# One f32 stack of a gated-attention/SSM mixer and an RWKV-7/sparse-attention block on one core: a three-stage join in the first mixer and four-corner matmuls in the state recurrence

## The chip, the cores and the metric

One Trainium2 chip, one NeuronCore in use. The metric is the device time of one execution in microseconds (us). TensorE (PE in the profile, with its weight loads as PEld), VectorE (DVE), ScalarE (ACT), GpSimd (POOL) and the queue of SyncE (SP) run their own instruction streams and meet on semaphores.

## The reference, cut to what matters

The change touches two parts. The first is the first mixer (512 tokens, 1024 channels), after its stick-breaking attention:

```python
proj = h @ w_in[layer]
q, k, v, z_attn, xbc, dt_raw, z_ssm = jnp.split(proj, splits, axis=-1)
...
y_attn = rms_norm(o, sb_norm_gain[layer]) * jax.nn.silu(z_attn)
xbc = jax.nn.silu(causal_depthwise_conv(xbc, conv_w[layer], conv_b[layer]))
dt = jax.nn.softplus((dt_raw + dt_bias[layer]).astype(jnp.float32))
y = ssd_scan(xs, dt, a, b_ssm, c_ssm, d_skip[layer])     # 4 chunks of 128 tokens, 16 heads
y_ssm = rms_norm(y * jax.nn.silu(z_ssm), ssm_norm_gain[layer])
mixed = jnp.concatenate([y_attn, y_ssm], axis=-1) @ w_out[layer]
x = x + gate[:, None, :] * mixed
```

`dt_raw`, the step sizes, is `h` times a 1024x16 part of the weights. The second is the recurrence of the RWKV-7 block (16 heads of 64 channels):

```python
def _wkv7_step(state, inp):
    r_t, w_t, k_t, v_t, a_t, b_t = inp
    sa = jnp.einsum('bhvk,bhk->bhv', state, a_t)
    state = (state * w_t[:, :, None, :] + sa[..., None] * b_t[:, :, None, :]
             + v_t[..., None] * k_t[:, :, None, :])
    y = jnp.einsum('bhvk,bhk->bhv', state, r_t)
    return state, y
```

The kernel computes it in 8 chunks of 64 tokens. Within a chunk the dependence of each token on those before it is a triangular 64x64 system for each head, and the kernel builds the inverse of its matrix in five levels of doubling.

## The kernel before

Everything lies in SBUF with channels on the 128 partitions, as tiles `F[i]` of 8 x 512 columns. Weights stream through `ring`, six slots of 512 KB that SyncE fills in a fixed `plan`; PE's `weight_used` frees a slot. All orders are written out by hand; no scheduler or planner moves an instruction.

**Split products.** Large f32 products run as three fp32r passes (`passes`, 128x512): weights and input are each split into a high part (a cast on ScalarE) and a low part (a subtraction). For one weight tile `t` of the joined first-mixer stream the chain is `high_of_weights(t)` on ScalarE into `w_high[t % 2]`, which has to wait until tile t-2 is done, then `low_of_weights(t)` (GpSimd from t = 2 on, L1337; VectorE for 0 and 1, L1244), then 24 passes on PE.

**The first mixer's stream (L1064 to L1343).** `w_dt` first: 32 f32 matmuls that hold 128 tokens of `h` as weights and stream 16 columns of `w_dt` (L1070). Then 12 convolution tiles, the first two interleaved by k, and 16 gate tiles `z_tile(j)`. The scan of four chunks is laid between gate tiles by `AFTER = [(1,2,3), (4,5,6), (7,8,9), (10,11,12)]`: chunk c's inputs, tile AFTER[c][0], its last broadcasts, the tiles AFTER[c][1] and AFTER[c][2], its outputs. ScalarE runs `chunk(c)` (its exponentials) whole and then `take_z` of the three tiles; `take_z(j)` also makes the high half of weight tile j+2. After `z_tile(13)` comes the sum of squares for the second norm, then tiles 14 and 15. GpSimd's `gate` multiplies the attention half by its gate.

**The output projection.** A new block `w_out` (`split_chain`, 16 weight tiles, 8 banks filled together). A block ends with a barrier of all engines; here ScalarE makes weights' and inputs' high halves, and VectorE both low halves and the final update of `x`.

**The recurrence (L1593 to L1846).** A round i handles chunks 2i and 2i+1 (x = 0, 1). `all_grams(i)` makes the Gram matrices and turns three tensors. Then for each level l: `q_level` (Q = N times G, L1663) for x = 0 and x = 1, and `g_level` for both: `GT += Q G`-like products into bank 3+2x (L1676) and, below level 5, `G`'s into bank 2+2x (L1680). Each is 8 pairs of heads x 2 halves = 16 f32 matmuls of 64x64, and each f32 matmul shows as two records in the profile, so 32 records. The two heads of a pair use partitions 0 to 63 and 64 to 127 of the inputs and the same of the output: two opposite corners of the array. VectorE takes every result (L1768 for Q, L1775 for GT, L1779 for G). Between the parts of the levels of round i stand the steps w, u, y, s of the previous round's two chunks (`carry`): w, u, y, s in levels 1 and 2, again in 3 and 4, none in level 5. GpSimd makes the start values (L1819 to L1823).

## Time and profile before

| | us |
|---|---|
| runs of the kernel before (3) | 2404.68, 2415.3, 2419.05; median 2415.3 |
| the profiled execution | 2409.52 |
| its span in the trace | 2407.7 |
| mean granted TensorE clock | 0.943 |

The profile is of one execution. Its span runs from the first to the last instruction of the program; the execution's own time is 1.8 us longer. Times of rows count from the start of the span. "Granted clock" is the share of the 2.4 GHz clock of TensorE: 1.0 is 2.4 GHz, 0.5 is 1.2 GHz. A matmul's end is modelled, so the distance from start to start says more of the rate than its duration.

### The profile page before, as it was taken

What the parts mean: (1) busy time and instruction counts of PE and PEld (TensorE: products, weight loads), DVE (VectorE), ACT (ScalarE), POOL (GpSimd) and SP (SyncE); (2) the same over time, 40 slices, a digit from 0 to 9 for tenths busy, and PEclk for the clock granted to TensorE, in tenths of its full rate; (3) what the DMA queues carried; (4) which work ended last, traced back from release to release, by engine and by line L of the source; (5) the groups of instructions that cost most, each with busy time, mean ns of one, the idle gap of its engine ahead of it and who ended that gap; (6) DMA issues with size and microseconds to landing.
All of it is one profiled execution on the core that took longest, in us unless ns stands there. A gap on an engine that the chain in (4) does not pass through costs nothing. (4 is left out here: it accounts for less than half of the span.)

```text
span 2407.7 us, 36981 instructions
## 1 busy us (share of the span) xinstructions
PE 2196.7 (91%) x16090; PEld 1677.4 (70%) x16090; DVE 1275.2 (53%) x1851; ACT 768.4 (32%) x1111; POOL 240.7 (10%) x171
## 2 busy tenths in 40 slices
PE   7998999988979966999899999899976988999898
PEld 3885777776858825999546788788434666888785
DVE  2335745554345475555435676733386536767434
ACT  2434653333223350000124222222244624222223
POOL 0000003233000043111310000000004400000000
PEclk9998989999989977999979999999887999999999
DMA  6221002111212200000101232322320021333231
GB/s 267 99 96 71 1 10 79 67 48 53 95 58 99 82 30 2 4 4 4 32 18 53 97 97 97 94 88 82 107 68 1 1 68 52 97 98 98 79 97 44
DMA packets 46850, 158.81 MB, mean 66 GB/s; under 512 B 5232, under 2 KB 7280, under 8 KB 46688
## 3 DMA queue, kind: packets, MB, share of 16 engines
q1 hardware_dynamic: 44832, 150.84, 19.1%
q10 hardware_dynamic: 1856, 5.60, 0.7%
q8 instruction: 127, 2.08, 0.3%
q14 instruction: 35, 0.29, 0.0%
HBM read 154.28 MB, written 2.14 MB: 65 GB/s over the span
## 5 line engine op out<-in xcount | busy, mean ns | idle before, releaser
L949 PE MATMUL banks<-up_x_high,up_w_high 128*128 128x512 f32 x672 | 262.1, 390 | 3.9 <-DVE up_w_low L920 3.9
L950 PE MATMUL banks<-up_x_low,up_w_high 128*128 128x512 f32 x672 | 262.1, 390 | 0.0
L951 PE MATMUL banks<-up_x_high,up_w_low 128*128 128x512 f32 x672 | 262.1, 390 | 0.0
L920 DVE TENSOR_TENSOR up_w_low<-weight_ring,up_w_high 128x1024 fp32r<-128x1024 f32 x88 | 107.8, 1226 | 129.8 <-ACT up_w_high L915 129.8
L915 ACT CAST up_w_high<-weight_ring 128x1024 fp32r<-128x1024 f32 x88 | 92.1, 1049 | 200.0 <-PE banks L951 171.7
L320 PE MATMUL banks<-down_x_high,down_w_high 128*128 128x512 f32 x352 | 139.1, 395 | 13.1 <-DVE down_x_low L359 13.1
L949 PEld LDWEIGHTS banks<-up_x_high,up_w_high 128*128 128x128 f32 x672 | 126.6, 188 | 30.9 <-issue 4.7
L951 PEld LDWEIGHTS banks<-up_x_high,up_w_low 128*128 128x128 f32 x672 | 126.6, 188 | 26.3
L950 PEld LDWEIGHTS banks<-up_x_low,up_w_high 128*128 128x128 f32 x672 | 126.4, 188 | 26.3
L321 PE MATMUL banks<-down_x_low,down_w_high 128*128 128x512 f32 x352 | 138.5, 393 | 0.0
L322 PE MATMUL banks<-down_x_high,down_w_low 128*128 128x512 f32 x352 | 138.4, 393 | 0.0
L357 DVE TENSOR_TENSOR down_w_low<-weight_ring,down_w_high 128x1024 fp32r<-128x1024 f32 x44 | 53.9, 1225 | 154.8 <-ACT down_w_high L341 154.8
L974 DVE SCALAR_TENSOR_TENSOR act<-banks,cols,act 128x511 f32<-128x511 f32 (+1 forms) x176 | 131.8, 749 | 6.3
L1337 POOL TENSOR_TENSOR hproj_w_low<-weight_ring,hproj_w_high 128x1024 fp32r<-128x1024 f32 x26 | 66.0, 2542 | 503.9 <-ACT hproj_w_high L1183 503.9
L1075 PE MATMUL banks<-hproj_x_high,hproj_w_high 128*128 128x512 f32 x224 | 93.5, 418 | 15.0 <-issue 12.0
L341 ACT CAST down_w_high<-weight_ring 128x1024 fp32r<-128x1024 f32 x44 | 46.2, 1049 | 174.8 <-PE banks L322 163.1
L1076 PE MATMUL banks<-hproj_x_low,hproj_w_high 128*128 128x512 f32 x224 | 91.0, 406 | 0.0
L1077 PE MATMUL banks<-hproj_x_high,hproj_w_low 128*128 128x512 f32 x224 | 90.7, 405 | 0.0
L320 PEld LDWEIGHTS banks<-down_x_high,down_w_high 128*128 128x128 f32 x352 | 67.1, 191 | 27.9 <-issue 13.9
L996 ACT ACTIVATE act<-act 128x512 f32<-128x512 f32 x44 | 27.8, 632 | 165.5 <-DVE act L974 165.5
L394 PE MATMUL banks<-rkv_x_high,rkv_w_high 128*128 128x512 f32 x192 | 75.3, 392 | 3.2 <-DVE rkv_x_low L456 3.2
L321 PEld LDWEIGHTS banks<-down_x_low,down_w_high 128*128 128x128 f32 x352 | 67.2, 191 | 14.1
(464 smaller groups left out, 4864.2 us busy)
## 6 DMA issues: line engine op xcount, KB each, us to landing
weight_ring<-in_up SPq DMA_DIRECT2D x88, 512.0 KB, 3.6
weight_ring<-in_down SPq DMA_DIRECT2D x44, 512.0 KB, 3.6
weight_ring<-in_w_ada SPq DMA_DIRECT2D x24, 512.0 KB, 5.9
weight_ring<-in_w_rkv SPq DMA_DIRECT2D x24, 512.0 KB, 3.2
weight_ring<-in_w_in SPq DMA_DIRECT2D x20, 512.0 KB, 3.6
weight_ring<-in_w_out SPq DMA_DIRECT2D x16, 512.0 KB, 3.2
weight_ring<-in_w_q SPq DMA_DIRECT2D x8, 512.0 KB, 6.3
weight_ring<-in_w_k SPq DMA_DIRECT2D x8, 512.0 KB, 3.2
```

Source lines behind the costliest of these rows:

```text
L320: nc.tensor.matmul(PS[:, n, :], high, x_high[:, k % 2, :], start=k == 0, stop=False)
L321: nc.tensor.matmul(PS[:, n, :], high, x_low[:, k % 2, :], start=False, stop=False)
L322: mm = nc.tensor.matmul(PS[:, n, :], low, x_high[:, k % 2, :], start=False, stop=last)
L915: nc.scalar.copy(w_high[:, n % 2, :], ring[:, i % RING, :]).then_inc(wh_made, 1)
L920: nc.vector.tensor_tensor(w_low[:, n % 2, :], ring[:, i % RING, :], w_high[:, n % 2, :].bitcast(f32), ALU.subtract).then_inc(wl_made, 1)
L949: nc.tensor.matmul(PS[:, n % 4, :], high, x_high[:, k, :], start=k == 0, stop=False)
L950: nc.tensor.matmul(PS[:, n % 4, :], high, x_low[:, k, :], start=False, stop=False)
L951: mm = nc.tensor.matmul(PS[:, n % 4, :], low, x_high[:, k, :], start=False, stop=k == 7)
L974: nc.vector.scalar_tensor_tensor(out=dst(n)[:, j:], in0=PS[:, n % 4, 0:T - j], scalar=w_col(n, taps - 1 - j), in1=dst(n)[:, j:], op0=ALU.m ...
L1075: nc.tensor.matmul(PS[:, bank, :], high, x_high[:, k, :], start=k == 0, stop=False)
L1076: nc.tensor.matmul(PS[:, bank, :], high, x_low[:, k, :], start=False, stop=False)
L1077: return nc.tensor.matmul(PS[:, bank, :], low, x_high[:, k, :], start=False, stop=k == 7)
```

## The change

In the first mixer: `w_dt` becomes the held operand (8 matmuls of up to 32 columns in four column groups of the array, k and k+4 adding up in one group, 512 tokens streamed), its partial sums are copied out and turned back by four small matmuls (`turn_dt`) that also add the four groups; convolution tiles 0 and 1 run one after the other; the low half of weight tile 1 moves from VectorE to GpSimd; in each scan chunk the high half for the tile AFTER[c][2] is made in the middle of ScalarE's chunk work; `z_tile(14)` goes ahead of the sum of squares; and the output projection's 16 tiles run in the same block, with the low half of the weights on GpSimd, `gate(pool, 15)` between the first two of them, and the scaling by the second norm between the input splits. In the recurrence: odd chunks use the two other corners of the array (their Q, GT and W lie with halves exchanged, so GpSimd makes their start value in `Q_[1]` and copies it across halves), the matmuls of Q and of G alternate between the two chunks, G is made before GT, and VectorE takes both G before both GT.

```diff
+        root, fix, eps_col = stat[:, 0, :], stat[:, 1, :], small[:, 250:251]
+        dt_rows, dt_halves, dt_picked = fix[0:112, :], late[0:112, 896:928], late[0:112, 928:944]
...
+        SPLIT_IN_CHUNK = [a[0] for a in AFTER]
...
-                for b in range(NB):
-                    for k in range(8):
-                        mm = nc.tensor.matmul(PS[:, 5, b * H:(b + 1) * H], h[:, k, b * P:(b + 1) * P], w[:, k * H:(k + 1) * H], start=k == 0, stop=k == 7)
+                for k in range(8):
+                    g = k % 4
+                    wide_cols = 32 if g < 3 else H
+                    mm = nc.tensor.matmul(PS[32 * g:32 * g + wide_cols, 5, :], w[:, k * H:k * H + wide_cols], h[:, k, :], start=k < 4, stop=k >= 4, skip_group_check=True)
                 mm.then_inc(weight_used, 1)
+
+                def turn_dt():
+                    pe.wait_ge(dt_step, 1)
+                    pe.wait_ge(dt_pick, 2)
+                    for b in range(NB):
+                        mm = nc.tensor.matmul(PS[:, 4, b * H:(b + 1) * H], dt_rows[:, b * P:(b + 1) * P], dt_picked, start=True, stop=True)
+                    mm.then_inc(dt_turned, 1)
...
+                        if j == 15 and k < 7:
+                            mm.then_inc(x_free, 1)
...
-                next_chunk(pe)
-                next_chunk(pe)
-                pe.wait_ge(wl_made, 2)
-                for k in range(8):
-                    pe.wait_ge(xl_made, k + 1)
-                    for t in range(2):
-                        mm = passes(t, k, t)
-                        if k == 7:
-                            mm.then_inc(weight_used, 1)
-                for t in range(2, N_XBC):
+                for t in range(N_XBC):
...
+                        if t == 0:
+                            pe.wait_ge(xl_made, k + 1)
                         mm = passes(t, k, t % 4)
                     mm.then_inc(weight_used, 1)
+                    if t == 0:
+                        turn_dt()
...
+                z_tile(14)
                 for i in range(8):
                     pe.wait_ge(s_squared, i + 1)
                     mm = nc.tensor.matmul(sum_bank, mat("ones"), sq_o(i), start=i == 0, stop=i == 7)
                 mm.then_inc(s_summed, 1)
-                z_tile(14)
                 z_tile(15)
+                for k in range(N_OUT):
+                    next_chunk(pe)
+                    pe.wait_ge(wl_made, N_TILES + k + 1)
+                    pe.wait_ge(out_xl, k + 1)
+                    last = k == N_OUT - 1
+                    for n in range(8):
+                        if k == 0 and n >= 6:
+                            pe.wait_ge(z_taken, 9 + n)
+                        high, low = (w[:, k % 2, n * P:(n + 1) * P] for w in (w_high, w_low))
+                        nc.tensor.matmul(PS[:, n, :], high, out_high(k), start=k == 0, stop=False)
+                        nc.tensor.matmul(PS[:, n, :], high, out_low(k), start=False, stop=False)
+                        mm = nc.tensor.matmul(PS[:, n, :], low, out_high(k), start=False, stop=last)
+                        if last and n < 7:
+                            mm.then_inc(out_made, 1)
+                    mm.then_inc(weight_used, 1)
...
-                    if j + 2 < 16:
+                    if j + 2 < 16 and j not in SPLIT_IN_CHUNK:
...
+                        if q4 == 1:
+                            high_of_weights(N_XBC + AFTER[c][0] + 2)
...
+                take_z(14)
+                high_of_weights(N_TILES)
                 act.wait_ge(s_summed, 1)
                 nc.scalar.activation(root, sum_bank, ACT.Abs_reciprocal_sqrt, bias=eps_col).then_inc(s_rooted, 1)
-                take_z(14)
+
+                def high_of_input(k):
+                    if k < 8:
+                        if k < 7:
+                            act.wait_ge(x_free, k + 1)
+                        else:
+                            tile_done(act, N_TILES - 1)
+                        act.wait_ge(z_gated, k + 1)
+                    else:
+                        tile_done(act, N_TILES + k - 8)
+                        act.wait_ge(s_scaled, k - 7)
+                    nc.scalar.copy(out_high(k), out_src(k)).then_inc(out_xh, 1)
+
+                high_of_input(0)
+                high_of_input(1)
+                high_of_weights(N_TILES + 1)
                 take_z(15)
+                for k in range(2, N_OUT):
+                    high_of_input(k)
+                    high_of_weights(N_TILES + k)
...
-                low_of_weights(1)
...
+                nc.vector.tensor_copy(dt_rows, PS[0:112, 5, :]).then_inc(dt_step, 1)
...
+                dve.wait_ge(dt_turned, 1)
+                nc.vector.tensor_tensor(by_block(z_), by_block(PS[:, 4, 0:64]), over_blocks("dt_bias"), ALU.add).then_inc(dt_step, 1)
+                dve.wait_ge(dt_step, 2)
+                nc.vector.tensor_scalar(m_, z_, 80.0, None, ALU.min).then_inc(dt_step, 1)
...
+                for k in range(N_OUT):
+                    dve.wait_ge(out_xh, k + 1)
+                    nc.vector.tensor_tensor(out_low(k), out_src(k), out_high(k).bitcast(f32), ALU.subtract).then_inc(out_xl, 1)
+                    if k < 8:
+                        nc.vector.scalar_tensor_tensor(out=y[:, k, :], in0=y[:, k, :], scalar=col("ssm_norm_gain", k), in1=root,
+                                                       op0=ALU.mult, op1=ALU.mult).then_inc(s_scaled, 1)
+                for n in range(8):
+                    if n < 7:
+                        dve.wait_ge(out_made, n + 1)
+                    else:
+                        tile_done(dve, N_TILES + N_OUT - 1)
+                    nc.vector.scalar_tensor_tensor(out=x[:, n, :], in0=PS[:, n, :], scalar=mod[:, 16 + n:17 + n], in1=x[:, n, :], op0=ALU.mult, op1=ALU.add)
...
+                for t in range(1, N_TILES):
+                    low_of_weights(t)
                     j = t - N_XBC - 2
                     if j >= 8:
                         gate(pool, j)
                 gate(pool, 14)
-                gate(pool, 15)
+                for k in range(N_OUT):
+                    low_of_weights(N_TILES + k)
+                    if k == 0:
+                        gate(pool, 15)
...
+        SAME, CROSS = tuple(zip(HALVES, HALVES)), tuple(zip(HALVES, HALVES[::-1]))
+        SIDES = (SAME, CROSS)
...
+                    for p in range(8):
+                        for x in range(2):
+                            nt = with_b[(2 * i + x) % 4].rearrange("p (h w) -> p h w", h=8)
+                            for half, side in SIDES[x]:
+                                mm = nc.tensor.matmul(PS[side, x, pair_cols(p)], nt[half, p, 0:LC], G_[x][half, pair_cols(p)], start=True, stop=True)
+                            if p == 7:
+                                mm.then_inc(q_made, 1)
...
+                    if l < LEVELS:
                         for p in range(8):
-                            for half in HALVES:
-                                mm = nc.tensor.matmul(PS[half, 3 + 2 * x, pair_cols(p)], Q_[x][half, pair_cols(p)], GT_[c % 4][half, pair_cols(p)], start=True, stop=True)
-                        if l < LEVELS:
-                            for p in range(8):
-                                for half in HALVES:
-                                    mm = nc.tensor.matmul(PS[half, 2 + 2 * x, pair_cols(p)], GT_[c % 4][half, pair_cols(p)], Q_[x][half, pair_cols(p)], start=True, stop=True)
+                            for x in range(2):
+                                c = 2 * i + x
+                                for half, side in SIDES[x]:
+                                    mm = nc.tensor.matmul(PS[half, 2 + 2 * x, pair_cols(p)], GT_[c % 4][side, pair_cols(p)], Q_[x][side, pair_cols(p)], start=True, stop=True)
+                                if p == 7:
+                                    mm.then_inc(gn_made, 1)
+                    for x in range(2):
+                        c = 2 * i + x
+                        for p in range(8):
+                            for half, side in SIDES[x]:
+                                mm = nc.tensor.matmul(PS[side, 3 + 2 * x, pair_cols(p)], Q_[x][side, pair_cols(p)], GT_[c % 4][side, pair_cols(p)], start=True, stop=True)
...
+                                for take in (take_g, take_gt) if part else (take_q,):
+                                    for x in range(2):
+                                        take(i, l, x)
...
+                    if x == 0:
+                        nc.gpsimd.tensor_tensor(by_pair(GT_[c % 4]), nt, over_pairs(first_mask_t), ALU.mult).then_inc(start_made, 1)
+                        pool.wait_ge(start_made, 8 * i + 2)
+                        nc.gpsimd.tensor_tensor(by_pair(GT_[c % 4]), by_pair(GT_[c % 4]), over_pairs(ident64), ALU.add).then_inc(start_made, 1)
+                    else:
+                        nc.gpsimd.tensor_tensor(by_pair(Q_[1]), nt, over_pairs(first_mask_t), ALU.mult).then_inc(start_made, 1)
+                        pool.wait_ge(start_made, 8 * i + 5)
+                        nc.gpsimd.tensor_tensor(by_pair(Q_[1]), by_pair(Q_[1]), over_pairs(ident64), ALU.add).then_inc(start_made, 1)
+                        pool.wait_ge(start_made, 8 * i + 6)
+                        for half, side in CROSS:
+                            nc.gpsimd.tensor_copy(GT_[c % 4][side, :], Q_[1][half, :]).then_inc(start_made, 1)
```

Three places where instructions move. First, ScalarE in the middle of scan chunk 0 (`scan0_vec` is VectorE's progress in the chunk; L1202/L1205 before are L1228/L1231 now, L1183 is L1209, L1189 is L1215). Before:

```order
L1202 ACTIVATE ssd_wide<-banks 128x512 [waits scan0_vec]
L1205 ACTIVATE ssd_wide<-ssd_wide 128x512 [waits scan0_vec]
L1202 ACTIVATE ssd_wide<-banks 128x512 [waits scan0_vec]
L1205 ACTIVATE ssd_wide<-ssd_wide 128x512 [waits scan0_vec]
L1189 ACT_TABLE_LOAD
L1189 ACTIVATE act4<-banks 128x512 [waits weight_used]
L1183 CAST hproj_w_high<-weight_ring 128x1024 [waits weight_used,weight_loaded4]
```

Now, from the same point:

```order
L1209 CAST hproj_w_high<-weight_ring 128x1024 [waits weight_used,weight_loaded4]
L1228 ACTIVATE ssd_wide<-banks 128x512 [waits scan0_vec]
L1231 ACTIVATE ssd_wide<-ssd_wide 128x512 [waits scan0_vec]
L1228 ACTIVATE ssd_wide<-banks 128x512 [waits scan0_vec]
L1231 ACTIVATE ssd_wide<-ssd_wide 128x512 [waits scan0_vec]
L1215 ACT_TABLE_LOAD
```

The cast of the weights in ring slot 4 stood behind the chunk's last exponentials, a table load and a gate tile's activation, and now stands ahead of them.

Second, ScalarE from the squares of the second norm to the output projection. Before:

```order
L1234 ACTIVATE ssd_wide<-act3 128x512 [waits norm_ssm_gated] x8
L1236 ACT_TABLE_LOAD
L1236 ACTIVATE stat<-banks,small 128x512 [waits norm_ssm_summed]
L1189 ACT_TABLE_LOAD [waits z_gated]
L1189 ACTIVATE aux<-banks 128x512 [waits weight_used]
L1189 ACTIVATE aux<-banks 128x512 [waits z_gated,weight_used]
L1064 UNCONDITIONAL_BRANCH
L241 UNCONDITIONAL_BRANCH [waits barrier_Pool_Activation_PE_DVE_SP_release]
L414 CAST w_out_w_high<-weight_ring 128x1024 [waits weight_loaded5]
```

Now:

```order
L1264 ACTIVATE ssd_wide<-act3 128x512 [waits norm_ssm_gated] x8
L1215 ACTIVATE aux<-banks 128x512 [waits z_gated,weight_used]
L1209 CAST hproj_w_high<-weight_ring 128x1024 [waits weight_used,weight_loaded5]
L1268 ACT_TABLE_LOAD
L1268 ACTIVATE stat<-banks,small 128x512 [waits norm_ssm_summed]
L1280 CAST hproj_x_high<-act2 128x512 [waits z_gated,hproj_x_free] x2
L1209 CAST hproj_w_high<-weight_ring 128x1024 [waits weight_used,weight_loaded0]
L1215 ACT_TABLE_LOAD [waits z_gated]
L1215 ACTIVATE aux<-banks 128x512 [waits weight_used]
```

The barrier is gone, the first output weight tile (slot 5) is split before the sum of squares is read, and the last gate tile's activation stands behind the split of the second.

Third, TensorE in one level of the recurrence, from Q on. Before (the instruction with the wait is the first of 16):

```order
L1663 MATMUL banks<-aux,rkv_act 64x64 [waits z_gated]
L1663 MATMUL banks<-aux,rkv_act 64x64 x15
...
L1676 MATMUL banks<-aux 64x64 x15
L1680 MATMUL banks<-aux 64x64 x16
L1676 MATMUL banks<-aux,late 64x64 [waits conv_silu]
L1676 MATMUL banks<-aux,late 64x64 x15
L1680 MATMUL banks<-late,aux 64x64 x16
```

Now (L1727 is Q, L1743 is G, L1750 is GT):

```order
L1727 MATMUL banks<-aux,rkv_act 64x64 [waits z_taken]
L1727 MATMUL banks<-aux,rkv_act 64x64 x31
...
L1743 MATMUL banks<-aux 64x64 x2
L1743 MATMUL banks<-late,aux 64x64 x2
...
L1750 MATMUL banks<-aux 64x64 x16
L1750 MATMUL banks<-aux,late 64x64 x16
```

Q's 32 matmuls now stand behind one wait for both chunks and G's go two by two between the chunks (`aux` is chunk 0's Q, `late` chunk 1's), while GT keeps 16 and 16.

## Rows read from the trace of the kernel before

**Rows 1.** The page: busy time of each engine.

```profile
PE 2196.7 (91%) x16090; PEld 1677.4 (70%) x16090; DVE 1275.2 (53%) x1851; ACT 768.4 (32%) x1111; POOL 240.7 (10%) x171
```

**Rows 2.** Busy time by stretch: tiles 0 and 1, recurrence; PEclk before the DMA share.

```profile
354.40:367.60 13.20, 13.16 (x48) 10.33 (x48) 2.02 (x4) 5.30 (x11) 0.00 (x0) 0.83 0.10 40
933.00:1173.70 240.70, 228.96 (x7616) 226.54 (x7616) 118.26 (x167) 18.73 (x32) 30.14 (x24) 0.99 0.02 4
```

**Rows 3.** Who TensorE waited for, 342 to 688: us, times, longest.

```profile
PE banks L1075 <- issue: 12.0, 4, 3.0
PE banks L394 <- DVE w_out_x_low L456: 5.3, 1, 5.3
PE banks L1075 <- POOL hproj_w_low L1337: 3.0, 1, 3.0
PE banks L1171 <- ACT ssd_wide L1234: 2.1, 1, 2.1
```

**Rows 4.** Timeline of the head: start, duration, engine, idle before.

```profile
342.78 11.59 PE L1070 MATMUL banks<-weight_ring,act 128*128 128x16 f32 x64 [0.95 <-PEq L736]
...
344.80 4.25 ACT L1211 CAST hproj_x_high<-act 128x512 fp32r<-128x512 f32 x8
...
346.26 4.90 DVE L1301 TENSOR_TENSOR hproj_x_low<-act,hproj_x_high 128x512 fp32r<-128x512 f32 x8
...
370.58 0.47 PE L1075 MATMUL banks<-hproj_x_high,hproj_w_high 128*128 128x512 f32 x1 [3.03 <-POOL hproj_w_low L1337]
```

**Rows 5.** Timeline of scan chunk 0, and a later low half without company.

```profile
446.62 1.95 PE L1094 MATMUL banks<-squares,late 128*128 128x128 f32 x16
...
449.84 4.90 DVE L1281 TENSOR_TENSOR ssd_wide<-ssd_wide,act 128x512 f32<-128x512 f32 x8
...
452.42 1.04 ACT L1183 CAST hproj_w_high<-weight_ring 128x1024 fp32r<-128x1024 f32 x1
...
453.54 3.40 POOL L1337 TENSOR_TENSOR hproj_w_low<-weight_ring,hproj_w_high 128x1024 fp32r<-128x1024 f32 x1 [11.95 <-ACT hproj_w_high L1183]
...
466.00 2.36 POOL L1337 TENSOR_TENSOR hproj_w_low<-weight_ring,hproj_w_high 128x1024 fp32r<-128x1024 f32 x1 [6.71 <-ACT hproj_w_high L1183]
```

**Rows 6.** Gate tiles by stretch: one before a stall, those behind the four.

```profile
448.30:454.04 5.74, 5.74 (x27) 4.43 (x25) 5.67 (x11) 5.00 (x7) 0.50 (x1) 1.00 0.17 67
457.05:464.35 7.30, 7.30 (x26) 5.60 (x28) 0.00 (x0) 0.00 (x0) 2.24 (x1) 0.77 0.00 0
...
sum 30.16, PE 30.16 PEld 23.18 DVE 0.00 ACT 0.00 POOL 12.68; mean PE 7.54 PEld 5.79 DVE 0.00 ACT 0.00 POOL 3.17
```

**Rows 7.** The seam to the output projection: timeline, and its first 6 us.

```profile
584.73 6.44 DVE L1330 SCALAR_TENSOR_TENSOR act<-act,cols,stat 128x512 f32<-128x512 f32 x8
...
597.99:603.99 6.00, 6.00 (x20) 4.84 (x21) 1.59 (x2) 0.00 (x0) 0.00 (x0) 0.73 0.00 0
```

**Rows 8.** Timeline of one level in round 0: TensorE, then VectorE.

```profile
958.44 1.15 PE L1663 MATMUL banks<-aux,rkv_act 64*64 64x64 f32 x32 [0.46 <-DVE aux L1779]
...
960.35 1.10 PE L1680 MATMUL banks<-aux 64*64 64x64 f32 x32
961.29 1.10 PE L1676 MATMUL banks<-aux,late 64*64 64x64 f32 x32
...
964.71 1.15 PE L1663 MATMUL banks<-aux,rkv_act 64*64 64x64 f32 x32 [0.46 <-DVE aux L1779]
...
961.50 0.69 DVE L1775 TENSOR_TENSOR aux<-banks,aux 128x512 f32<-128x512 f32 x1 [1.17 <-PE banks L1680]
```

**Rows 9.** Four column groups and two: matmuls (1292 to 1296), weight loads.

```profile
L497 PE MATMUL banks<-act,squares 128*32 128x512 f32 x16 | 1.9, 596 | 1.0 <-PEq L230 1.0
464.28 0.20 PEld L1127 LDWEIGHTS banks<-ssd_wide,act 128*64 128x64 f32 x4 [0.35 <-issue]
```

**Rows 10.** G's records under way at 960.355, and at 960.362: start, duration.

```profile
960.35 0.22 PE L1680 MATMUL banks<-aux 64*64 64x64 f32 x1
960.35 0.23 PE L1680 MATMUL banks<-aux 64*64 64x64 f32 x2
```

83 lines of the change are left out of this document (35 added, 48 removed).

## The prediction

> **What bounds the kernel now.** First the busy time of the engines: TensorE is busy for 91% of the span, VectorE for 53% [rows 1], so time is won only where TensorE's work shrinks, runs in parallel, runs at a higher clock, or waits less. Then the busy time by stretch: the 48 passes of the first two convolution tiles fill their 13.2 us, at a granted clock of 0.83; the recurrence takes 240.7 us, of which TensorE is busy 228.96 [rows 2]. There the reader is to see that few waits are left, so that a gain must come from the matmuls themselves. Then who TensorE waited for in the first mixer: four gaps of 3.0 in the scan chunks, 3.0 ahead of convolution tile 2, 2.1 at the sum of squares, 5.3 at the seam to the output projection [rows 3]. Timelines of these places follow, part by part.
>
> **Head of the stream.** The 64 f32 records of w_dt take 11.59 us, from 342.78 to 354.37; the two tiles end with the stretch at 367.6; tile 2 waits 3.03 for its low half and starts at 370.58 [rows 2, 4]. Now w_dt is 8 matmuls, 16 records, in four column groups. Such records exist: 16 of 128x512, four groups, take 1.9 us together at 596 ns each [rows 9], so four rounds and not sixteen; 2 to 3.5 us here, by the clock. That ends before tile 0 can start, which needs the first low half of the input: ScalarE's first cast starts at 344.80 and takes 4.25/8 = 0.53, VectorE's subtraction 4.90/8 = 0.61 behind it [rows 4], so about 346.3. From there the same 48 passes at 13.2 us and the turn (8 f32 records behind a copy, estimated at 0.9, less than a tenth of the 64 records' time) end at 360.4, a gain of 10.2. At the full clock the passes would take 13.2 x 0.83 = 11.0, and the gain be 12.4. The low half of tile 2 now has the whole of tile 1 to be made in (1.04 cast, 2.36 GpSimd [rows 5], against at least 5.5), so the 3.03 goes, and is counted in those numbers. GpSimd's low half for tile 1 is ready about 353, one us before tile 0 ends. I take 11.0, since the long stretch of 128x16 matmuls at the front is gone; ends 10 and 12.5.
>
> **The four scan chunks.** The chunk's first gate tile ends about 446.6, when the tile-after-next's slot is free, but ScalarE casts only at 452.42, behind its exponentials; GpSimd subtracts for 3.40 from 453.54, where the same instruction takes 2.36 alone [rows 5]. The gate tile between ends at 454.04 [rows 6] and TensorE idles 3.0 [rows 3]. Behind the gap the tile runs in 7.54 on the mean of four, against 5.74 at the full clock [rows 6]: 1.8 more each. Now the cast comes right behind the first tile: 446.8 to 447.9. GpSimd starts at 447.9 and has 1.9 us of its 2.36 done when VectorE's eight products begin at 449.84; they last to 454.74 [rows 5], both operands in SBUF. In the row of 3.40 the overlap with them was 454.74 - 453.54 = 1.2 and cost 1.04, so GpSimd nearly stands still beside them. It thus ends between 450.3 (no blocking) and 454.74 + 0.46 = 455.2, or 455.9 if an earlier VectorE operation blocks it too. Wanted at 454.04: a new gap of 0 to 1.9; I take 1.0. Does the clock still fall behind it? It fell behind gaps of 3.0 and 5.3 [rows 3, 6, 7]; a gap of 1.0 is nearer to none, so I take the 1.8 back. Per chunk 3.0 - 1.0 + 1.8 = 3.8, four chunks **15.2**; ends 4 x 2.0 = 8.0 (the clock falls all the same) and 4 x 4.8 = 19.2. Queued behind the early cast on ScalarE are the last exponentials, 1.04 later, which chunk outputs need; they also need VectorE's products, which set their time.
>
> **The seam.** z_tile(14) takes the place of the 2.1 wait for the squares [rows 3]. The norm's root and VectorE's eight scalings used to stand between (6.44 from 584.73 [rows 7]); now they are spread over the first output tiles, each under the 5.7 of a tile. The 5.3 gap [rows 3] goes, since the first output tile's weights and inputs are ready before z_tile(15) ends, and with it the low clock behind it: 6.00 at 0.73 is 1.6 [rows 7]. New: ScalarE casts the second output tile's weights only when tile 15 is done (1.04 [rows 5]), then loads a table and runs the last activation (estimated 1.9 together, from the 5.3 of the old seam, in which the same pieces lay), GpSimd runs gate 15 (estimated 1.3, since a 2.36 low half has twice its columns) and then the low half, 2.36 [rows 5]: 6.6, with the hand-overs 6.8, against 5.5 of an output tile without waits (13.2 x 0.83 for 48 passes, half of it [rows 2]), a stall of about 1.3, up to 2.6 with GpSimd slowed as above. Sum 2.1 + 5.3 + 1.6 - 1.3 = **7.7**, ends 6.4 and 9.0. The steady chain of the other 14 tiles, 1.04 + 2.36 up to 3.40, stays under a tile. What follows the projection is as before.
>
> **The recurrence.** 32 records of G start at 960.35 and the next group at 961.29 [rows 8]: 29 ns from start to start for one chunk's two corners. Two records of opposite corners start within 10 ns (0.22 for one, 0.23 for two [rows 10]) and the next pair 58 later, so a corner is what is busy, not the issue. Column groups run beside each other in the same way, and four weight loads of two column groups lie within 0.20 [rows 9]. With the other two corners Q of both chunks, 64 records, should take 0.93 instead of 1.87, and G the same. GT is not interleaved and stays 1.87.
> Round 0 has no other work between the levels, so the chain counts. Before: 964.71 - 958.44 = 6.27 from one level's second Q to the next's [rows 8], six groups of 0.93, a 0.46 wait and what lies before it. After, counted from Q's start: Q 0.93; VectorE takes the two Q at 0.69 each [rows 8], 1.61 with an estimated 0.25 for the hand-over, so G starts at 2.54 and ends at 3.47; GT follows to 5.34, and both G are taken by 5.1. Period 5.34, saving 0.93 in each of four levels (level 5 has no G and gains nothing), less 0.5 for the first level, which now waits for both chunks' start: 3.2.
> In rounds 1 to 3 the w, u, y, s steps of the previous chunks stand between the parts and hide VectorE's takes, so the matmul time itself counts: 4 levels x 1.87 (0.93 for Q and for G) = 7.5, less 0.7 where the second chunk's w waits for the state, less 0.5 for level 5: 6.3, three times 18.9. Sum **22.1**; ends 18.5 (nothing in round 0) and 25.7 (those 1.2 not lost). GpSimd's two copies for the odd chunk's start value are under 1.3 each and end some 1.5 us ahead of the first Q; its total is only 240.7 us, 10% [rows 1]. Priced at nothing.
>
> **Sum.** 11.0 + 15.2 + 7.7 + 22.1 = 56.0. The profiled execution took 2409.5, so 2353.5 in its terms; it lies 5.8 below the median of 2415.3, so **2359**. With all terms at their ends 42.9 to 66.4 are saved: 2349 to 2372.
>
> **Rivals.**
> *Deeper overlap.* If TensorE also runs GT of chunk 1 beside GT of chunk 0 (one group of 16 matmuls behind the other), another 5 x 4 x 0.46 = 9.3 goes, and with the chunk gaps gone 4.0: 2346. Against it: records of one group are issued in order, and those of the next start only as it ends [rows 8]. Chance 0.10.
> *Issue is the limit.* The pairs' spacing may be set by the rate at which TensorE takes records, and four corners then give little. The change puts Q and G of both chunks, (320 + 256) x 4 = 2304 records, into common groups; VectorE then no longer takes one chunk while TensorE works on the other, which costs 1.87 + 1.61 + 1.87 + 1.87 = 7.22 against 6.27 a level, 4.6 in round 0, and an estimated 1.0 in each other round, where other work hides it: 7.6. At an unchanged 29.2 ns the recurrence is 7.6 slower and the total 2415.3 - 33.9 + 7.6 = 2389; at 21.9, half-way to the 14.6 I forecast, 2304 x 7.3 = 16.8 comes back: 2372. The middle is 2380. Rows 10 speak against it, rows 9 only for column groups. Chance 0.20. The Trainium skill, page "TensorE: Matmul & The Clock Gate", section "Wait — 56ns, not 53.3ns?", says that starts never come closer than about 25 ns; by it the saving would be 4.2 x 2304 = 9.7 and the time 2379. The two starts within 10 ns disagree with it.
> *Slower: corners that share rows or a bank exclude each other.* In the new order a chunk's corner and the other chunk's share 64 rows of the array or 64 columns. If such two can't run at once, and switching costs a turn each, the spacing rises from 29.2 to the 58.3 of one corner: 2304 x 29.2 = 67 more, and the 7.6: 2415.3 - 33.9 + 74.9 = 2456. It decides from (33.9 - 7.6) / 2304 = 11.4 ns above 29.2, 40.6 per record. For it: nothing in the trace shows all four corners at once. Against: column groups do share rows [rows 9]. Chance 0.04. The Trainium skill, page "TensorEngine Tiling (Array Packing)", "Gotcha 1: PSUM Pressure", says that different row tiles can't access one PSUM bank at once; each chunk's two corners already do, and start within 10 ns [rows 10], so this trace does not bear it out.
> *The mixer's gaps stay.* If GpSimd is stopped for the whole of VectorE's work and the clock falls again in each chunk, 3.0 - 1.9 = 1.1 is saved per chunk, 10.8 less than forecast; with a stall of 1.0 at each of 16 output tiles, and a recurrence that saves 9.2 as at 21.9 ns, 56.0 - 10.8 - 16 - 12.9 = 16.3 is left: 2399. Chance 0.04.
>
> **How the numbers follow.** The forecast has 0.62, the others 0.10, 0.20, 0.04, 0.04. A range of 2340 to 2386 takes in the forecast's own, the deeper overlap and most of the issue case; left out are its top, the slower case and the last. About 1% (24 us) is what a measurement of this kernel tells from no change, so faster means under 2391: 0.62 + 0.10 + 0.17 = 0.89; within 1% 0.07, slower 0.04.
>
> **What the profile after would show.** Convolution tile 2 starting near 359.5; under 1.9 ahead of the tiles AFTER[c][2], with those tiles near 5.7; output tile 0 directly behind tile 15 and a gap near 1.3 ahead of output tile 1; 64 records of Q or G in about 1.15 from first start to last end; the level period in round 0 at 5.3 instead of 6.27; the recurrence near 219 instead of 240.7. Wrong would be a Q group of 2 us (issue or exclusion), or TensorE waiting for GpSimd's low halves at many output tiles: that engine has no spare time if VectorE's work slows it everywhere.

## The result, and the profile after

| | us | ratio to before | 95% interval |
|---|---|---|---|
| kernel before (4 runs) | 2414.7 | | |
| changed kernel (4 runs) | 2383.3 (2374.6 to 2386.5) | 0.9882 | 0.9855 to 0.991 |

Of the four runs of the mixer part alone, below, one was slow (3191.7 us at a granted clock of 0.643), and the other three have a median of 2380.2.

Faster by 1.2%, inside the range of 2340 to 2386, but with little more than half of the 56 us that were forecast. The profiled execution has a span of 2382.0, 25.7 below the 2407.7 of before. Its span and the busy time of its engines, against [rows 1]:

```profile
span 2382.0 us, 36961 instructions
PE 2158.5 (91%) x16050; PEld 1637.4 (69%) x16050; DVE 1291.0 (54%) x1837; ACT 769.1 (32%) x1111; POOL 287.2 (12%) x196
```

TensorE is 38.2 us less busy and the span only 25.7 shorter: waits have been added. Who TensorE waited for in the first mixer and the output projection answers to [rows 3]:

```profile
PE banks L1089 <- DVE hproj_x_low L1354: 3.4, 1, 3.4
PE banks L1195 <- issue: 1.9, 1, 1.9
PE banks L1089 <- ACT aux L1215: 1.3, 3, 0.4
...
PE banks L1089 <- ACT act L1215: 0.4, 1, 0.4
```

The four gaps of 3.0, the 3.0 ahead of tile 2, the 2.1 and the 5.3 are gone. What is left is the wait for the first low half of the input, 1.9 ahead of the second output tile, and 0.4 four times ahead of the tiles in the scan chunks. The timeline of the head, against [rows 4]:

```profile
340.48 1.92 PE L1077 MATMUL banks<-act,weight_ring 128*32 128x512 f32 x16 [0.95 <-PEq L736]
345.81 0.47 PE L1089 MATMUL banks<-hproj_x_high,hproj_w_high 128*128 128x512 f32 x1 [3.42 <-DVE hproj_x_low L1354]
...
353.00 0.96 PE L1084 MATMUL banks<-late,stat 112*128 112x16 f32 x8
353.81 0.47 PE L1089 MATMUL banks<-hproj_x_high,hproj_w_high 128*128 128x512 f32 x1
```

Counted from w_dt's first record, tile 2 comes 18.9 us later (359.37, the start of tile 2's first pass), against 27.8 before: 8.9 won. Windows of a gate tile with its gap, of the tile behind it, and of the first output tile, against [rows 6, 7]:

```profile
437.04:443.20 6.16, 5.72 (x28) 4.44 (x26) 6.09 (x9) 4.35 (x7) 2.07 (x1) 1.00 0.17 65
443.20:449.20 6.00, 6.00 (x31) 4.78 (x33) 2.07 (x4) 1.55 (x3) 2.96 (x1) 1.00 0.26 87
561.15:567.15 6.00, 5.61 (x25) 4.32 (x23) 2.56 (x3) 3.74 (x5) 2.70 (x2) 1.00 0.26 87
```

A gate tile and the gap behind it take 6.16 in place of 8.73, and the clock stands at 1.00 in all three. The recurrence is another matter. Its window in the kernel before, from the first Gram record to the last of GT, and then the changed kernel's:

```profile
933.87:1153.90 220.03, 214.82 (x7174) 213.19 (x7176) 112.94 (x159) 17.56 (x30) 30.14 (x24) 0.99 0.02 4
```

```profile
897.53:1125.31 227.78, 194.14 (x7175) 188.38 (x7177) 112.97 (x159) 17.58 (x30) 34.99 (x32) 0.96 0.02 4
```

TensorE does the same records in 20.7 us less busy time, and the stretch is 7.8 us longer: its idle time went from 5.2 to 33.6. The granted clock differs too, 0.96 against 0.99. The late-cast kernel below has the same code in this stretch, and in its profile the clock was 0.99:

```profile
913.90:1133.80 219.90, 187.66 (x7175) 182.24 (x7177) 112.78 (x159) 17.59 (x30) 35.03 (x32) 0.99 0.02 4
```

So at an equal clock the stretch takes what it took before, with 27 us less busy time and 27 us more idle time. Who TensorE waited for in the changed kernel's recurrence (the largest lines):

```profile
PE banks L1750 <- DVE late L1838: 7.7, 4, 2.0
PE banks L1750 <- issue: 6.5, 7, 1.5
PE banks L1743 <- DVE late L1838: 5.6, 4, 1.6
PE banks L1727 <- issue: 3.0, 4, 1.1
```

18 of the 33 us end with VectorE (the lines of 7.7 and 5.6, and two of 2.4 and 1.9), and 15.4 end with "issue", that is, with nothing that this view shows. The second kind did not exist in the recurrence before. The timeline of the second level in round 0 shows both, against [rows 8]:

```profile
917.55 0.27 PE L1743 MATMUL banks<-aux 64*64 64x64 f32 x2 [1.43 <-DVE late L1838]
...
920.37 1.13 PE L1727 MATMUL banks<-aux,rkv_act 64*64 64x64 f32 x58
922.00 0.33 PE L1727 MATMUL banks<-aux,rkv_act 64*64 64x64 f32 x4 [0.51 <-issue]
923.32 0.27 PE L1743 MATMUL banks<-aux 64*64 64x64 f32 x2 [0.99 <-DVE late L1838]
```

Q's group runs at the forecast pace: 58 records in 1.13 (with 0.22 for the last one, 16 ns from start to start). Then TensorE stops in the middle of the group, ahead of four records that no semaphore holds back. Counting the trace's records from 914 us on, such stops stand ahead of records 1559, 1686, 1813, 1940, 2068, 2195 and so on to 2704: 127 or 128 apart. The queues' summary of the recurrence gives a cause to test: q8 fetches instructions, in 57 DMAs for 7175 records, 126 records each.

```profile
DMA packets 59, 0.95 MB, mean 4 GB/s; under 512 B 0, under 2 KB 0, under 8 KB 0
...
q8 instruction: 57, 0.93, 1.8%
```

The single packets of q8 tie the two together. The stop at 922.00 ends 1.31 behind the end of a fetch (919.45 to 920.69), the one at 926.75 ends 1.36 behind the next (924.42 to 925.39), and so with each of the 23 stops by "issue" in the changed kernel's recurrence: 1.2 to 1.5 us behind the end of a fetch.

### The profile page after: what moved, and what is told of

It reads as the page before. It is cut to its first block and busy times, and to the rows that moved or that the text cites. A ratio compares the mean times of both kernels' runs of the same rounds, so it can differ in the third digit from the quotient of the medians.

```text
span 2382.0 us, 36961 instructions
## 1 busy us (share of the span) xinstructions
PE 2158.5 (91%) x16050; PEld 1637.4 (69%) x16050; DVE 1291.0 (54%) x1837; ACT 769.1 (32%) x1111; POOL 287.2 (12%) x196
## 5 line engine op out<-in xcount | busy, mean ns | idle before, releaser
L1401 POOL TENSOR_TENSOR hproj_w_low<-weight_ring,hproj_w_high 128x1024 fp32r<-128x1024 f32 x43 | 105.5, 2455 | 509.2 <-ACT hproj_w_high L1209 509.2
L996 ACT ACTIVATE act<-act 128x512 f32<-128x512 f32 x44 | 27.8, 632 | 164.3 <-DVE act L974 164.3
L322 PEld LDWEIGHTS banks<-down_x_high,down_w_low 128*128 128x128 f32 x352 | 67.3, 191 | 14.4
```

The costliest lines, as they stand in the source:

```text
L322: mm = nc.tensor.matmul(PS[:, n, :], low, x_high[:, k % 2, :], start=False, stop=last)
L1401: nc.gpsimd.tensor_tensor(w_low[:, t % 2, :], ring[:, (first + 1 + t) % RING, :], w_high[:, t % 2, :].bitcast(f32), ALU.subtract).then_inc ...
```

## The experiments

Two theories stood against each other for the recurrence. **Supply:** TensorE's instructions arrive in blocks of 128 records, one in some 3.8 us, and four corners use them up in half that time. **Dependencies:** the shorter groups no longer cover VectorE's takes. Times of the recurrence below are those of one profile each, from its first Gram record to the last GT; its records are those that the window shows, a few of neighbouring groups included.

| kernel | us, median of all runs | ratio (95%) | recurrence | records | TensorE idle in it |
|---|---|---|---|---|---|
| before | 2414.7 | | 220.0 | 7174 | 5.2 |
| changed | 2383.3 | 0.9882 (0.9855 to 0.991) | 227.8 | 7175 | 33.6 |
| half the instructions in Q, G | 2361.1 | 0.9797 (0.9773 to 0.982) | 205.9 | 6021 | 17.4 |
| twice the instructions in Q, G | 2451.0 | 1.0175 (1.0148 to 1.0201) | 295.0 | 9479 | 54.7 |
| mixer part only | 2380.6 | 0.9873 (0.9851 to 0.9895) | 220.7 | 7174 | 5.4 |
| new order, two corners | 2389.3 | 0.9913 (0.9886 to 0.9941) | 228.2 | 7175 | 14.0 |
| merged Grams | 2377.3 | 0.9862 (0.9835 to 0.9888) | 219.7 | 6663 | 31.9 |
| merged Grams, level 5 in turn | 2377.0 | 0.9854 (0.9824 to 0.9883) | 218.2 | 6662 | 27.5 |
| mixer part, merged Grams | 2376.2 | 0.9857 (0.9831 to 0.9884) | 219.5 | 6662 | 5.5 |
| late cast in the chunks | 2392.9 | 0.9925 (0.9903 to 0.9947) | 219.9 | 7175 | 32.2 |

**The rate by itself.** Ahead of the recurrence of the kernel before, records that nothing waits for:

```diff
+                piece = lambda rows, p, w=HD: squares[rows, p * w:(p + 1) * w]
...
+                for r in range(16):
+                    for p in range(8):
+                        for bank, rows, side in ((0, LO, LO), (0, HI, HI), (1, LO, HI), (1, HI, LO)):
+                            nc.tensor.matmul(PS[side, bank, p * HD:(p + 1) * HD], piece(rows, p), piece(rows, p + 1), start=True, stop=True)
```

> The kernel before, with 3072 extra f32 records put ahead of the recurrence, which nothing waits for or feeds: 256 in one corner, 256 in two corners that share rows, 256 in two that share columns, 1024 in four corners of 64x64 with 64 columns streamed, 512 in four corners with 128 columns, 512 in two opposite corners. Theory supply (TensorE gets its instructions in blocks of 128 records, and no faster than one block per about 3.8 us, the pace at which the blocks' DMAs follow each other in the recurrence of both kernels): the 1024 records start 14.6 ns apart until the blocks that were already there are used up, then halt at every 128th record and come at about 29.7 ns on average, 27 to 30 us in all; the 512 with 128 columns take the same 29 ns each, 15 us, without a halt. Theory dependencies (the lost time of the recurrence is waits for VectorE, and TensorE itself runs four corners at 14.6 ns for as long as wanted): the 1024 records take 15 us with no halts. One corner should show 58 ns in both.

The timeline of TensorE in the run of four corners with 64 columns:

```profile
979.86 3.53 PE L1616 MATMUL banks<-squares 64*64 64x64 f32 x211
984.75 2.09 PE L1616 MATMUL banks<-squares 64*64 64x64 f32 x128 [1.36 <-issue]
988.20 2.10 PE L1616 MATMUL banks<-squares 64*64 64x64 f32 x128 [1.36 <-issue]
991.93 2.10 PE L1616 MATMUL banks<-squares 64*64 64x64 f32 x128 [1.63 <-issue]
995.66 2.09 PE L1616 MATMUL banks<-squares 64*64 64x64 f32 x128 [1.63 <-issue]
999.66 2.10 PE L1616 MATMUL banks<-squares 64*64 64x64 f32 x128 [1.91 <-issue]
1003.67 2.09 PE L1616 MATMUL banks<-squares 64*64 64x64 f32 x128 [1.91 <-issue]
```

The rows need no arithmetic: 128 records in 2.09, idle, 128 records, idle, with no semaphore anywhere. Inside a block the records are 14.7 ns apart (2.09 less 0.22 over 127): the four corners do run side by side. From block to block it is 3.45 to 4.01 us, 3.73 on the mean of seven (from 981.30, inside the first row, to 1007.39), and that is 29 ns per record, the very pace of two corners. The packets of q8 follow the same beat: a fetch takes 0.9 to 1.3 us, TensorE starts the block 1.3 to 1.5 behind its end, and the next fetch starts 1.05 to 1.66 behind that. These three add up to the period. The 1024 records took 28.4 us, as supply had it. Pairs that share rows or share columns ran two at a time as well (54 ns per record at half the clock, where one corner had 107, and 29 at the full clock). I was wrong on the start: there was hardly a store to run down, since the first short stop came after 87 records and the first long one after 215. I was wrong on one corner too: it ran at half the clock all the time and took 107 ns, so its 58 at the full clock was not seen. The 128-column run, forecast without a halt, had three, of 1.1 down to 0.3 us from start to start, before it kept pace.

**Other lengths.** The same with 128, 32, 256 and 96 columns.

> The kernel before with four runs of f32 records in four corners ahead of the recurrence, that nothing waits for: 512 records of 128 columns, 1024 of 32 columns, 192 of 256 columns, 512 of 96 columns. Theory supply: the period of a block of 128 records is its own, 3.5 to 4.0 us, whatever the array needs: with 32 columns (7.3 ns a record, 0.93 us a block) halts of 2.6 to 3.0 us at every block, with 96 columns (22 ns, 2.8 us) halts near 1, with 128 (29 ns, 3.7 us) none or small ones, and the 256-column records, 58 ns, let the store fill again, so that the first block or two of the 96-column run have no halt. If the halts instead followed the work (a pause of 1.6 to 2.1 us after each 128 records), the 32-column blocks would take 2.5 to 3.0 us and the 96-column ones 4.5 to 5.

```profile
954.42 3.62 PE L1610 MATMUL banks<-squares 64*64 64x32 f32 x214
959.70 3.23 PE L1610 MATMUL banks<-squares 64*64 64x32 f32 x128 [1.66 <-issue]
963.43 3.64 PE L1610 MATMUL banks<-squares 64*64 64x32 f32 x128 [0.50 <-issue]
967.43 15.47 PE L1610 MATMUL banks<-squares 64*64 64x32 f32 x553 [0.36 <-issue]
...
993.75 5.94 PE L1618 MATMUL banks<-squares 64*64 64x96 f32 x278
1000.07 2.87 PE L1618 MATMUL banks<-squares 64*64 64x96 f32 x128 [0.38 <-issue]
1003.80 2.52 PE L1618 MATMUL banks<-squares 64*64 64x96 f32 x106 [0.86 <-issue]
```

With 96 columns, 20.6 ns a record, the first halt comes only after 278 records, but not because so much was in store: the 278 are the last 22 of a block and two blocks more, and q8 fetched the second of these (994.18 to 995.06) while the 96-column run, which began at 993.75, was on its way. After the slow 256-column run some 150 records were there, the rest of a block and one more. Then blocks start 3.7 us apart, as with 64 columns. The period is the supply's own, and the pause is what is left of it. With 32 columns a record did not get shorter (14.7 ns at first; then the granted clock fell to 0.5 and records came at 26 to 27 ns, so that the halts shrank): the 7.3 ns and the halts of 2.6 to 3.0 that were expected did not come. A smaller matmul is no faster here, which matters for the next but one run.

**Half the instructions.** In the changed kernel, with all waits kept; the real Q and G are left out (Q's edit, G's is like it):

```diff
-                            for half, side in SIDES[x]:
-                                mm = nc.tensor.matmul(PS[side, x, pair_cols(p)], nt[half, p, 0:LC], G_[x][half, pair_cols(p)], start=True, stop=True)
+                            for part in range(2):
+                                mm = nc.tensor.matmul(PS[:, x, pair_cols(p)], b16[:, 0:P], b16[:, 0:HD], start=part == 0, stop=part == 1)
```

> The changed kernel, in which each chunk's Q and G of a pair of heads are two accumulating 128x128 bf16 matmuls on constants in place of four f32 records in two corners: half the instructions (1152 records fewer in the recurrence) in about the same array time, with all semaphores, waits and VectorE work as they were. It leaves out the real Q and G. Theory supply: the recurrence falls from 227.8 us by the halts that no semaphore ends (15.4) and up to 1152 x 29.7 ns = 34, so the kernel takes 2349 to 2368. Theory dependencies: VectorE's chain is the same, so the recurrence stays at 225 to 230 and the kernel at 2380 to 2386.

Measured 2361.1, the recurrence 205.9 at a clock of 0.98, in supply's range; that is 14.0 under the 219.9 at 0.99. All of TensorE's waits in it, apart from the start:

```profile
PE banks L1751 <- DVE late L1839: 7.4, 4, 1.9
PE banks L1744 <- DVE late L1839: 5.9, 4, 1.5
PE banks L1686 <- DVE aux L1854: 2.4, 3, 0.8
PE banks L1764 <- DVE stat L1873: 1.6, 3, 0.5
```

Not one wait by "issue" is left, while the waits for VectorE are what they were (17.3). A Q group of both chunks takes 1.11 here (32 records), as in the changed kernel, so array time was kept. Dependencies had 225 to 230 here, and falls as the cause of the 15 us. It is left with the waits for VectorE, of which 5.2 were there before the change.

**Twice the instructions.** The same work in half-width matmuls (Q's edit, G's is like it):

```diff
-                            for half, side in SIDES[x]:
-                                mm = nc.tensor.matmul(PS[side, x, pair_cols(p)], nt[half, p, 0:LC], G_[x][half, pair_cols(p)], start=True, stop=True)
+                            for part in range(2):
+                                at = slice(p * HD + 32 * part, p * HD + 32 * part + 32)
+                                for half, side in SIDES[x]:
+                                    mm = nc.tensor.matmul(PS[side, x, at], nt[half, p, 0:LC], G_[x][half, at], start=True, stop=True)
```

> The changed kernel, in which each 64-column matmul of Q and G is two of 32 columns: the same array time if a record's time follows its columns, and 2304 records more. Theory supply: 18 more blocks of 128 records at 3.8 us, +68 us, less what falls into waits for VectorE (about 18): 2433 to 2452. Theory dependencies: within 5 us of the changed kernel's 2383. A plain floor of 25 ns per record, with no blocks, would give + 2304 x 25 = 58 as well, but with starts never closer than 25 ns and no halts.

Measured 2451.0, +67.2 in the recurrence. But the run on lengths shows that the premise of equal array time doesn't hold: 2304 records at 14.7 ns are 34 us of array by themselves. Waits by "issue" rose from 15.4 to 41.5:

```profile
PE banks L1729 <- issue: 14.1, 15, 1.9
...
PE banks L1747 <- issue: 12.7, 11, 1.8
PE banks L1754 <- issue: 6.6, 7, 1.6
```

The granted clock in the recurrence was 0.93 too, the lowest of all, which adds to the time. So it agrees with supply (74 instruction DMAs, at 3.8 us each 281 of the 295 us) and doesn't prove it as the half kernel does.

**The mixer part alone**, with the old recurrence:

> The changed kernel with the recurrence of the kernel before: the first mixer's and the output projection's part of the change alone. Both theories: the mixer keeps its 34.5 us, and the recurrence takes 220.0 in place of 227.8, with the granted clock at 1.0 in it; 2414.7 - 34.5 = 2380 at the least gain and 2383.3 - 7.8 = 2375 at the best, so 2373 to 2381, faster than the changed kernel by 2 to 10 us. If the four corners had won time and the mixer lost it, this would be slower than the changed kernel.

Measured 2380.6, ratio 0.9873, within the interval of the changed kernel's 0.9882; in the profile the recurrence has 220.7. The whole of the measured gain is the mixer's. The expected 2 to 10 us between the two are there in the medians (2.7) and not beyond the intervals.

**The new order with two corners:**

```diff
-        SIDES = (SAME, CROSS)
+        SIDES = (SAME, SAME)
```

> The changed kernel with its new order in the recurrence (Q and G alternating between the chunks, G ahead of GT, both G taken before both GT), but the odd chunk in the same two corners as the even one. Theory supply (blocks of 128 records' instructions, one per 3.5 to 3.8 us at best): two corners take 29 ns per record, which is the pace of the supply, so nothing is lost by giving the other two corners up; 214.8 us of matmuls, 5 more in round 0 for the lost overlap and 1.6 at each level 5 make about 226, and the kernel takes 2379 to 2387, the same as the changed one. Theory dependencies (the four corners did win their 33 us and new waits for VectorE ate them): those waits are as long with slower groups ahead of them, so the recurrence takes 245 to 260 and the kernel 2400 to 2415.

The recurrence takes 228.2, as supply had it, and is 8.2 longer than before, which was the price set in the prediction for the lost overlap (7.6). The window of the recurrence:

```profile
901.30:1129.50 228.20, 214.21 (x7173) 212.94 (x7175) 113.12 (x159) 17.56 (x30) 34.98 (x32) 0.99 0.02 4
```

Set against the profile of the changed kernel (227.8) the other two corners give nothing; set against another profile of the very same recurrence, in the late-cast kernel (219.9, clock 0.99 in place of 0.96), they give 8, and the medians have 6, with intervals that overlap. The second comparison is at equal clock. So four corners win back what the new order costs, and no more. The kernel's 2389.3 is above the 2379 to 2387 expected by that. Its idle time is a reading of its own: 14.0, all of it waits for VectorE and none by "issue". So of the rise of these waits from 5.2 to 17.6 in the changed kernel, 8.8 come with the new order and 3.6 with the shorter groups.

**Fewer instructions, all computed.** Gram matmuls that share a weight are merged:

```diff
-                        for j, right in enumerate(rights):
-                            for half in HALVES:
...
-                                mm = nc.tensor.matmul(dst, of_head(left, p, half, c), of_head(right, p, half, c), start=True, stop=True)
+                        for half in HALVES:
+                            dst = PS[half, bank + at0 // 8, at0 % 8 * LC:(at0 % 8 + n) * LC]
+                            right = of_head(rights[0], p, half, c) if n == 1 else acts[half, 1:5:3, p, c * LC:(c + 1) * LC]
+                            mm = nc.tensor.matmul(dst, of_head(left, p, half, c), right, start=True, stop=True)
```

> The changed kernel, computing all of it, with 512 records fewer in the recurrence: where a Gram matmul streams two tensors against one weight, one matmul of 128 columns takes the place of two of 64 (two activation tiles exchange places so that one access reaches both). Array time and waits are as in the changed kernel. Theory supply: 4 blocks fewer at 3.8 us, 15 us at most, of 15.4 us of halts; the Gram stretches hold no halts themselves, but they leave blocks in store for what follows: 5 to 15 us less, 2368 to 2378. Theory dependencies: no change, 2383 within 3.

> As the kernel with merged Gram matmuls, and at level 5, which has no G, the two chunks' Q one after the other, so that GT of the first chunk needs only the first take. The wait ahead of GT at level 5 (2.0 us three times, 1.6 once) should fall by the length of a take, 0.65 each: 2 to 3 us less than the merged kernel by both theories, if the supply isn't what ends there.

> The mixer part of the change with the recurrence of the kernel before and the merged Gram matmuls. Here each record occupies its corner longer than a record of the supply takes, so theory supply expects no gain from fewer instructions: 2377 to 2383, as without the merging (2380.6). If merging helped here as much as it does with four corners, it would work by something else than the supply.

The recurrences take 219.7, 218.2 and 219.5. Against 227.8 the first would be the 8 us expected, but against 219.9 at an equal clock it is nothing, and the three medians (2377.3, 2377.0, 2376.2) can't be told from each other or from 2380.6. Waits by "issue" stayed at 13.7 in the first. The run on lengths says why: little more than one block is in store, so blocks saved in the Gram stretch, which has no halts, are of no use ten microseconds later. Only instructions saved inside a stretch of four corners count. In the second kernel the waits for VectorE at level 5 fell from 7.7 to 1.5, and "issue" rose by 2 (13.7 to 15.8); 1.5 us are left in the recurrence of the 6. The third is no slower than the four-corner kernels: none of these beats the mixer part with the old recurrence.

**The early cast undone:**

```diff
-        SPLIT_IN_CHUNK = [a[0] for a in AFTER]
+        SPLIT_IN_CHUNK = []
...
-                        if q4 == 1:
-                            high_of_weights(N_XBC + AFTER[c][0] + 2)
```

> The changed kernel without the early cast in the scan chunks: the high half for the tile behind each chunk's gap is made after the chunk's last exponentials, as before. The four gaps of 3.0 us come back and, if the low clock behind them was theirs, the tiles behind them take 7.5 in place of 5.7: 4 x (3.0 + 1.8 - 0.4) = 17.6 us more, 2399 to 2401. If the gain in the chunks came from elsewhere (the joined stream, say), 2383 to 2387. If the gaps come back and the clock does not fall, about 10 more, 2393.

The four gaps are back, and the clock behind the first of them too, but not behind all:

```profile
PE banks L1089 <- issue: 12.0, 4, 3.0
```

```profile
447.71:454.98 7.27, 7.27 (x26) 5.57 (x26) 0.00 (x0) 0.00 (x0) 2.23 (x1) 0.77 0.00 1
```

From z_tile(1) to z_tile(13) it takes 121.6 us, against 108.0 in the changed kernel and 125.7 before. 13.6 are lost: four times 8.72 - 6.16 = 2.56 at the gaps, and 1.6 behind each of the two gaps that left the clock low. Before, it was low behind all four. The medians have 9.6 (2392.9 against 2383.3), at the 10 of gaps alone. The gaps are shown to be the cast's; how often a gap of 3.0 costs the clock varies.

## Why the prediction was right or wrong

**Head, 11.0.** Right in kind, 8.9 measured. The four column groups took 1.92 and turn_dt 0.96, as said; the two tiles with turn_dt took 13.6 (345.81 to 359.37), a little less than the 14.1 (13.2 and 0.9) that stand for the low clock. What was missed is ahead of them: tile 0 starts 5.3 after w_dt, not 3.5. GpSimd's low half of tile 1 was expected to be held back by VectorE until 353; it got in first, and VectorE stood still:

```profile
342.68 2.44 POOL L1401 TENSOR_TENSOR hproj_w_low<-weight_ring,hproj_w_high 128x1024 fp32r<-128x1024 f32 x1 [342.26 <-ACT hproj_w_high L1209]
343.15 6.73 DVE L1354 TENSOR_TENSOR hproj_x_low<-act,hproj_x_high 128x512 fp32r<-128x512 f32 x8 [0.25 <-ACT hproj_x_high L1239]
```

The eight subtractions took 6.73 in place of 4.90 [rows 4]. The excess is all in the first, for which tile 0 waits: 1.8 of the 2.1 missing.

**Scan chunks, 15.2.** 17.6 measured (125.7 to 108.0). The same exclusion worked the other way round from the forecast:

```profile
436.72 2.39 POOL L1401 TENSOR_TENSOR hproj_w_low<-weight_ring,hproj_w_high 128x1024 fp32r<-128x1024 f32 x1 [6.40 <-ACT hproj_w_high L1209]
437.16 2.23 DVE L1326 TENSOR_SCALAR ssd_wide<-ssd_wide 128x512 f32<-128x512 f32 x1
...
440.02 0.43 DVE L1326 TENSOR_SCALAR ssd_wide<-ssd_wide 128x512 f32<-128x512 f32 x1
```

GpSimd ran at its full 2.4 and VectorE's 0.43 took 2.23, so its products came 1.8 later (440.37) and GpSimd never met them. The gap ahead of the tile is 0.44 in place of 1.0, and what ends it is ScalarE's reading of the bank, not the low half. The clock came back in all four, as taken.

**Seam, 7.7.** 7.9 measured up to the first output tile (31.27 from z_tile(13) to it before, 23.35 now), and 89.3 for the 16 output tiles against 88.8, where the new stall (1.9, 1.3 in the forecast) takes back a little more than the recovered clock (1.6) gives: 7.4 in all. The mixer together: 34.0 against 33.9 forecast, from the first record of w_dt to the end of the last of w_out. (The 34.5 in the expectation of the mixer part is half a microsecond too much.) That the sum comes out so well is in part luck, for the head fell short by 2.1 and the chunks gave 2.4 too much.

**The recurrence, 22.1.** This is the step that failed; profiles of its code have 227.8 and 219.9 against 220.0, so nothing was won. Three sentences of it:
"With the other two corners Q of both chunks, 64 records, should take 0.93": right. The 58 records in 1.13 and the 14.7 ns of the rate run show it.
"Period 5.34": the first was 5.77 (917.55 to 923.32), with 0.51 of halt in it, later ones 6.3.
"In rounds 1 to 3 ... the matmul time itself counts": wrong twice. At 14.7 ns TensorE wants a block of 128 records each 1.9 us and gets one each 3.7, so over half of the time won in Q and G was spent in halts in the same or the following groups: 15.4 us, all of which went when these groups had half the instructions. And the new order together with the shorter groups left more of VectorE's takes uncovered than I allowed for: waits that end there rose from 5.2 to 17.6, at G and at GT of level 5, where no carry step stands between. For level 5 I had set down 0.5 a round; GT there waits 2.04 in each of rounds 1 to 3, against 0.31 before. Most of the rise (8.8 of 12.4) is the order's, as the run with two corners shows, a cost that the rival had priced at 7.6 and the forecast itself only in round 0. (The rival's 4.6 for round 0 is more than four levels at 7.22 - 6.27 give, 3.8.) Together: 27 us of busy time less, at equal clock, and 27 us more idle. The distance of 29 ns that I read as "a corner is what is busy" was also the pace of the blocks, 3.75 us for 128 records in the old recurrence, and nothing in the rows of before could tell the two apart. The Trainium skill, page "Runtime: NRT & Kernel Launch", section "Instruction fetch mechanics", says that instructions are refilled in blocks of 16 KiB or 256, at a cost that is mostly hidden. The block agrees with this trace (0.93 MB in 57 DMAs; a record is a weight load and a matmul); that it is hidden held for the kernel before and not for this one.

**The rivals.** "Issue is the limit" was nearest in time (2380 for 2383), and its description, that TensorE takes records no faster, is half right: starts are as close as forecast, and the mean over a block is what is capped. Exclusion of corners is out: all four ran together, in pairs on one bank too. Low halves held up no output tile but the second, by the 1.9 above (568.62, behind a GpSimd run that began at 564.45).

**What stays open.** How much longer four corners take by the clock: the changed kernel's profile has 19 us at half the clock inside the recurrence, the late-cast kernel's 5. Beyond the first 5 to 6 us of the recurrence, the two merged kernels with four corners have 3.4 each at half the clock, and the four kernels with two corners there have none; but with one profile each a cause isn't shown. Nor is it shown what a fetch waits for before it starts.

## What to carry to other kernels

Before packing small matmuls side by side, count instructions, not only array time: here TensorE got 128 f32 records (a weight load and a matmul each) per 3.7 us, about 29 ns each, and work packed tighter than that stops in the middle of a group with "issue" as the releaser, each 128 records. Four corners should pay if a matmul is long (an estimate: with 128 columns they ran at 27 to 29 ns a record, at which the blocks keep up; two corners with 128 columns weren't run), or for short bursts behind slow stretches; a saving of instructions counts only in the stretch that is starved. And when groups are made shorter or put in another order, look at them as cover: ask whose results they were hiding.

## What the runs showed of the hardware

- Four 64x64 corners of TensorE run at once in f32, also two that share rows and two that share columns: 14.7 ns from start to start on the mean with 64 columns at the full clock, which is 59 within a corner. One corner alone took 107 at half the clock.
- 32 columns in four corners are no faster than 64: 14.7 ns.
- Instruction blocks of 128 records (16 KB, one DMA of q8) arrive 3.45 to 4.0 us apart under demand. TensorE starts on one 1.3 to 1.5 us behind the end of its DMA, and the next DMA starts 1.05 to 1.66 us behind that (rate run). After a slow stretch some 150 records are in store.
- GpSimd's 128x1024 subtraction and VectorE's operations on SBUF held each other up, and in the three places looked at the one that was under way first went through: VectorE's 0.43 became 2.23 and its first subtraction 1.8 longer; in the kernel before it was GpSimd that stood still (3.40 for 2.36).
